# Splitting 1024-column weight units whole, the low part stored over the raw unit, in a one-layer diffusion block on Trainium2

## What is computed

```
mod = silu(c) @ w_ada + b_ada                       # six vectors: sh1 sc1 g1 sh2 sc2 g2
h   = modulate(rms_norm(x), sh1, sc1);  hc likewise for ctx
p   = h @ w_in ; pc = hc @ w_in                     # q, k, v of both head groups, rotary
x   = x + g1 * (concat(diff_attention, window_attention) @ w_out)
h2  = modulate(rms_norm(x), sh2, sc2)
q   = h2 @ peer_w_q ; top 16 of 128 x 128 keys per head -> experts, gates
x   = x + g2 * sum_e gate * gelu(h2 . u_e) * v_e
out = rms_norm(x)
```

## Time and profile before

| what | value |
|---|---|
| median of 3 runs | 2382.22 us (2380.1 to 2387.5) |
| the profiled execution | 2381.41 us |
| its span in the trace | 2379.6 us |
| PE busy | 2252.3 us, 95% of the span |
| DVE busy | 1640.9 us, 69% |
| ACT busy | 1220.5 us, 51% |
| POOL busy | 248.0 us, 10% |
| DMA | 453 MB, mean 190 GB/s |

### The profile page before, as it was taken

One profiled execution on the slowest core, in us unless ns is written; L12 is line 12 of the kernel. 1 busy time (PEld: TensorE's weight loads), 2 busy tenths in 40 slices (PEclk: granted clock), 3 DMA queues, 4 the chain that ended last, 5 costly groups with the idle time before them and its releaser, 6 DMA issues.

```text
span 2379.6 us, 43735 instructions
## 1 busy us (share of the span) xinstructions
PE 2252.3 (95%) x14034; PEld 1975.0 (83%) x14034; DVE 1640.9 (69%) x2935; ACT 1220.5 (51%) x2195; POOL 248.0 (10%) x152
## 2 busy tenths in 40 slices
PE   4899999579997999999999999999999999999997
PEld 1488887356897999999999999999888888888886
DVE  6387667776668878888868887877555555555555
ACT  2232244256444367677665555555555555555554
POOL 0000000920004610000111111111000000000000
PEclk8899999689998999999999999999999999999999
DMA  9878867310475745555554444444655555565552
GB/s 381 344 259 280 287 236 249 131 36 1 141 250 192 239 156 180 185 180 181 187 167 159 159 159 159 159 158 151 229 191 192 192 192 194 194 194 193 193 191 102
DMA packets 123895, 453.29 MB, mean 190 GB/s; under 512 B 14401, under 2 KB 15169, under 8 KB 123201
## 3 DMA queue, kind: packets, MB, share of 16 engines
q1 hardware_dynamic: 123840, 452.63, 56.3%
HBM read 448.38 MB, written 4.19 MB: 190 GB/s over the span
## 4 chain that ended last, share of the span: by engine, by line
PE 88%; DVE 7%; DMA 2%; issue 2%; ACT 1%; SPq 0%; DVEq 0%; ACTq 0%
PE PS L683 78%; PE PS L956 2%; PE PS L837 2%; DVE w_lo L1034 2%; DMA ada_t<-w_ada 1%; PE PS L811 1%; DVE pr L1258 1%; DVE st L1256 1%; PE PS L725 1%; PE PS L690 1%; PE PS L825 1%; PE PS L666 1%; DMA raw<-stream 1%; DVE yb L1070 0%; DVE st L1232 0%
## 5 line engine op out<-in xcount | busy, mean ns | idle before, releaser
L1034 DVE TENSOR_TENSOR w_lo<-raw,w_hi 128x512 fp32r<-128x512 f32 x1296 | 924.8, 723 | 566.5 <-ACT w_hi L373 551.2
L373 ACT ACTIVATE w_hi<-raw 128x512 fp32r<-128x512 f32 x1296 | 815.9, 630 | 912.6 <-PE PS L683 899.1
L683 PE MATMUL PS<-h_h,w_hi 128*128 128x256 f32 (+1 forms) x2304 | 661.7, 287 | 14.3 <-DVE w_lo L1034 14.3
L683 PE MATMUL PS<-h_l,w_hi 128*128 128x256 f32 (+1 forms) x2304 | 654.1, 284 | 0.0
L683 PE MATMUL PS<-h_h,w_lo 128*128 128x256 f32 (+1 forms) x2304 | 653.9, 284 | 0.0
L683 PEld LDWEIGHTS PS<-h_h,w_hi 128*128 128x128 f32 x2304 | 444.3, 193 | 16.9 <-DVE w_lo L1034 9.0
L683 PEld LDWEIGHTS PS<-h_l,w_hi 128*128 128x128 f32 x2304 | 444.6, 193 | 0.1
L683 PEld LDWEIGHTS PS<-h_h,w_lo 128*128 128x128 f32 x2304 | 444.2, 193 | 0.0
L683 PE MATMUL PS<-w_hi,p_hi 128*128 128x512 f32 x1024 | 398.5, 389 | 0.0
L683 PE MATMUL PS<-w_lo,p_hi 128*128 128x512 f32 x1024 | 398.3, 389 | 0.0
L683 PE MATMUL PS<-w_hi,p_lo 128*128 128x512 f32 x1024 | 398.3, 389 | 0.0
(11 more groups left out here) (192 smaller groups left out, 2465.3 us busy)
## 6 DMA issues: line engine op xcount, KB each, us to landing
raw<-stream SPq DMA_DIRECT2D x648, 512.0 KB, 3.4
ada<-w_ada SPq DMA_DIRECT2D x128, 512.0 KB, 4.6
ada_t<-w_ada SPq DMA_DIRECT2D x64, 512.0 KB, 9.5
x_c<-x_ctx SPq DMA_DIRECT2D x1, 2048.0 KB, 7.9
x<-x_lat SPq DMA_DIRECT2D x1, 2048.0 KB, 15.1
x_scratch<-x SPq DMA_DIRECT2D x1, 2048.0 KB, 7.3
x<-x_scratch SPq DMA_DIRECT2D x1, 2048.0 KB, 10.6
outT<-ot SPq DMA_DIRECT2D x4, 512.0 KB, 2.6
```

Of the source, the lines that this page charges most:

```text
L373: nc.scalar.activation(w_hi[:, (2 * j + hf) % SPLIT, :], raw[:, j, hf * HALF:(hf + 1) * HALF], ACT.Copy).then_inc(S["w_high"], 1)
L683: ins = mm(out_, l_, r_, start=(start and q == 0), stop=(stop and q == 2), skip_group_check=check)
L1034: V_.tensor_tensor(w_lo[:, h % SPLIT, :], raw[:, h // 2 % RAW, at_:at_ + HALF], w_hi[:, h % SPLIT, :].bitcast(F32), ALU.subtract).then_inc ...
```

## The change

ACT rounds a whole unit (1024 columns) in one instruction, and DVE makes its low part in one instruction. The low part is written over the raw unit: `w_lo` now lies at the address of `raw`. The memory that `w_lo` had goes to `w_hi`, so both rings hold eight halves (four units). Because the raw slot now holds the low part until PE has read it, SP issues the load of unit u only when PE has used unit u-4 (`w_free`), no longer when the low part of unit u-4 is made. The places where a half was split for each row or each third of a step (`modulate_and_split`, `next_low`) now split a unit at every second half.

```diff
-RAW, SPLIT, ADA, ADA1 = 4, 4, 4, 8
+RAW, SPLIT, ADA, ADA1 = 4, 8, 4, 8
...
-        w_lo = at("w_lo", [P, SPLIT, HALF], F32R, 24 * KB)
+        w_lo = at("w_lo", [P, SPLIT, HALF], F32R, 0)
...
                 if not first:
-                    sp.wait_ge(S["w_low"], 8 * b + 2 * (j - 3))
+                    sp.wait_ge(S["w_free"], 8 * b + 2 * (j + 1))
                 sp.dma_start(raw[:, j, :], stream[4 * b + j]).then_inc(raw_in[j], 16)
...
-            def half_high(b, j, hf):
-                act.wait_ge(S["w_free"], 8 * b + (2 * j + hf + 1))
-                nc.scalar.activation(w_hi[:, (2 * j + hf) % SPLIT, :], raw[:, j, hf * HALF:(hf + 1) * HALF],
-                                     ACT.Copy).then_inc(S["w_high"], 1)
-
             def split_high(b, j):
 
                 act.wait_ge(raw_in[j], 16 * b + 16)
-                half_high(b, j, 0)
-                half_high(b, j, 1)
+                act.wait_ge(S["w_free"], 8 * b + 2 * (j + 1))
+                nc.scalar.activation(w_hi[:, 2 * j:2 * j + 2, :].rearrange("p a n -> p (a n)"), raw[:, j, :], ACT.Copy
+                                     ).then_inc(S["w_high"], 2)
...
                 if k % 2 == 0:
-                    act.wait_ge(raw_in[k // 2 % RAW], 16 * (k // 8) + 16)
-                half_high(k // 8, k // 2 % RAW, k % 2)
+                    split_high(k // 8, k // 2 % RAW)
...
             def split_low(b, j):
-                half_low(b, 2 * j)
-                half_low(b, 2 * j + 1)
+
+                dve.wait_ge(S["w_high"], 8 * b + 2 * (j + 1))
+                V_.tensor_tensor(w_lo[:, 2 * j:2 * j + 2, :].rearrange("p a n -> p (a n)"), raw[:, j, :],
+                                 w_hi[:, 2 * j:2 * j + 2, :].rearrange("p a n -> p (a n)").bitcast(F32), ALU.subtract
+                                 ).then_inc(S["w_low"], 2)
...
                 modulate_low(k)
-                half_low(k // 8, k % 8)
+                if k % 2 == 0:
+                    split_low(k // 8, k // 2 % RAW)
...
                 for _ in range(n):
-                    half_low(half[0] // 8, half[0] % 8)
+                    if half[0] % 2 == 0:
+                        split_low(half[0] // 8, half[0] // 2 % RAW)
                     half[0] += 1
```

## The result

| what | before | changed |
|---|---|---|
| median | 2381.19 us of 4 runs (2380.1 to 2387.5) | 2404.86 us of 4 runs (2401.5 to 2409.44) |
| ratio | | 1.0095, 95% interval 1.0068 to 1.0123: slower, by about 1% |
| span of the profiled execution | 2379.6 us | 2406.0 us |

The page of the changed kernel: busy time by engine, then its two groups of splits (count, busy us, mean ns, idle before and its releaser; the ones to set beside them are in the earlier trace rows).

The account below looks back on a forecast made before the run. PE was taken to bound the kernel, busy 95% of the span. Terms 3.0 - 1.0 + 13.7 - 7.5 + 2.6 + 0.5 = +11.3 us on 2381.4 gave 2392.7, plus 0.8 for the median, rounded to 2394; range 2382 to 2403.

Parts of the forecast that it names:

- First chunk, +3.0: First chunk: PE's first half waits longer for a fresh whole unit in four groups; +3.0 us (1.5 to 4).
- Chunks 5 to 8, -1.0: Chunks 5 to 8: the deeper ring lets rotary work start earlier at chunk ends; -1.0 us (-2.5 to +1.5).
- Output projection, +13.7: Output projection: late `ada` load and sum delay low parts; PE stalls seven times 1.95 us, +13.7 us (10.9 to 18.6).
- The next pair arrives in time: Output projection: the pair after a stall was released before it, so the 1.95 us stall comes once in four units.
- Query projection, -7.5 and +2.6: Query projection: wider DVE turns and fewer waits, -7.5 us (-2 to -12); POOL's late last `ada` load at its end, +2.6.
- the 4.4 us: Query projection: what the wider DVE instruction recovers over some 40 halves that took 1.55 us against PE's 1.44.
- U and V, +0.5: U and V stages: 5.9 us to a ready unit fits in 8.2 us with little to spare; +0.5 us (0 to 3).
- Attention, 0: Attention, up to the first matmul of the output projection: forecast 0 us.
- the loose ring: Rival: `ada` lands in about 3.3 us, output projection term falls to 5; total +3, 2385 us; chance 0.22.
- The lock turns: Rival: 1024-column turns free the query projection of its waits, gaining some 20 us; about 2376 us; chance 0.08.
- loads did not bound the long stages: Denies the rival that landing over 6 us makes every ring slot late in the long stages: 2446 us; chance 0.05.

Follow-up runs that it names:

- e2: Kernel before, still with 512-column splits, but low part over the raw unit, rings of four units, load released by PE; 2390.84 us, ratio 1.0042.
- e6: Changed kernel with output projection `ada` loads one turn earlier, first chunk split by halves, `x2` read back in four pieces; 2375.97 us, ratio 0.9969.
- e3: Changed kernel with each `ada` load of the output projection one turn (two units) earlier in SP's queue; 2382.71 us, ratio 1.0006.
- e7: e3 with the `ada` loads of the query projection one turn earlier too; 2383.92 us, ratio 1.0.
- e4: Changed kernel with DVE's sum behind the two low parts of its turn in the output projection, SP's queue unchanged; 2382.11 us, ratio 1.0004.
- e5: e2 with the edit of e3, and `x2` read back in four pieces; 2374.28 us, ratio 0.9971.
- e8: e3 with the first four `ada` loads of column group 5 ahead of the loads of units 74 and 75; 2387.4 us, ratio 1.0014.
- e1: Kernel before with 1024-column splits, low parts in their own buffer, rings of two units, load released by the low part; 2492.73 us, ratio 1.0476.

## Why the prediction was wrong

The direction, the stage and the mechanism of the largest term were right; the size was half of what was measured, and the time (2404.86) fell just above the range (2382 to 2403). The output projection's term was too small by 8.0 us, more than half of the 15 us that are missing. By the steps of the prediction:

- **First chunk, +3.0: right.** Measured +3.1, shown to be the width's by e2 and e6.
- **Chunks 5 to 8, -1.0: the sign right, the size open.** It was -2.6. PE's wait for the turned queries fell from 6.2 to 4.2 us, and to 3.9 with halves (e2), so the gain of the deeper ring is there and larger than the 0.9 that I gave it. But e3, e7 and e4, which have the changed kernel's code there, show -2.4, -2.6 and +0.2; the granted clock of the stage was 0.96 in e4, 1.00 in the other three and 0.97 before the change. One trace does not settle a term of this size.
- **Output projection, +13.7: this is the step that failed, in size.** The period and the count held: the 28 units from 76 on are seven groups of four, and their waits are 1.79, 2.40, 2.18, 2.40, 2.08, 2.52 and 2.24 us, 2.23 in the mean where I had 1.95. That is 1.9 us in all. (By the prediction's own numbers the pair behind a stall has no slack, 7.7 us against 1.95 + 5.77. So between units 80 and 90 the loss of a group is split over its two pairs: 1.69 and 0.71, 0.82 and 1.36, 0.26 and 2.14. "The next pair arrives in time" was not right there, without changing the sum of a group.) The parts are not all right either: in the turn shown above the `ada` load left 0.86 us after PE's end with unit 77 (642.68), where I had 0.5, and landed in 4.2 us, where I had 4.5. The larger error is that a stall was priced at its length alone: the edges of ten waits are 2.5 us, and the lower clock behind three of them, less what the start of the stage lost before the change too, 4.1. Together these are 8.5 us for the 8.0 that the term was short. The prediction quoted the clock of 0.77 behind the gaps of the query projection and used it only for a rival; the term put both at nothing.
- **Query projection, -7.5 and +2.6: the sum near (-3.6 against -4.9), both parts wrong, which is luck.** PE's waits for low parts fell only from 14.3 to 11.0 us, and 2.0 of that came from the large stalls, where I had counted 3.1 (4.63 and 6.93 us before; 2.46, 2.64 and 4.46 now). The same code gave -6.5 in e3 and -5.6 in e4 for the norm and this stage. I expected that a DVE turn between two of GpSimd's would carry twice as many columns in the same time. The trace after, DVE first, then GpSimd:

```profile
809.13 58.59 DVE L1028 TENSOR_TENSOR w_lo<-raw,w_hi 128x1024 fp32r<-128x1024 f32 x19 [2.02 <-ACT w_hi L375]
```

```profile
811.08 3.27 POOL L346 TENSOR_TENSOR acc<-acc,ada 128x1024 f32<-128x1024 f32 x1
```

  19 units in 58.59 us are 3.08 us each. Before, 24 halves in 37.23 were 3.10 for a unit. GpSimd's sum, 2.70 us before, now takes 3.27, as it stands behind a longer instruction. The turns got wider for both, and the 4.4 us were not recovered. The late end cost nothing either: PE waited 1.9 us for the copies of the result, as before. The Trainium skill, SBUF — State Buffer, section "Who interferes with whom", says that the port pair which VectorE and GpSimd share is an exclusive lock, held for the whole of the instruction that came first; the trace agrees, now with GpSimd's 3.27 us as the number.
- **U and V, +0.5: low.** U was +0.2, with 0.6 us of waits for low parts in it. V was +2.3, of which 1.9 is the wait behind the read of `x2`, a DMA in SP's queue that I had not counted among the things that a unit load is late behind. That e5 and e6 bring the stage to +0.1 shows it.
- **Attention, 0:** +2.8 here, and between -1.6 and +3.5 in e3, e4 and e7 with the same code, so no finding about the change. The tail's +1.6 is 0.0 in e3, e4 and e7 and 1.7 in e8, whose code there is the same; its granted clock was 0.81 here and 0.86 before the change, and I read it the same way.

Of the rivals, the loose ring fell: `ada` landed in 4.1 us (median of 15, from 3.9 to 4.6), 0.4 less than before the change, and not in 3.3. The Trainium skill, SBUF — State Buffer, section "The DMA setup-cost knee", by whose fit the transfer alone would take an estimated 3.2 us, comes close for the unit loads of this kernel (3.3 by the page of the profile), and not for the `ada` load that follows two of them (4.1). The lock turns did not decide, and loads did not bound the long stages.

With the output projection's term as measured, 21.7 us, the prediction's sum is +19.3 us where the trace has +26.4. The 7.1 us that are left are U and V (2.0 more than forecast), the query projection (1.3), chunks 1 to 4 (0.9), the first chunk (0.1), and attention and tail (4.4), which differ between executions of one code, less 1.6 of chunks 5 to 8.

## What to carry to other kernels

When a buffer is written in place, its load is released by the last reader instead of the middle one, and everything that stands behind that load in the same queue moves with it: look there for another transfer that an engine needs before its next step on the buffer. Break such a dependency where the slack is cheapest; here moving each load, or each sum, by a turn gave back all 21.7 us. A wider instruction delays its first result and holds up the engine it excludes for longer, and in e1 it did not pay in a ring of two units. A wait of PE is priced with its edges and with the slower matmuls that may follow it: here 2.5 and 4.1 us beside 15.6.

## What was not expected of the hardware

- Behind three of ten PE waits, of 1.79, 2.52 and 2.24 us, the granted clock fell to 0.50 for 3.4 us; behind the other seven, of up to 2.14 us, it stayed at 1.00 through 75 us.
- The same code with the same busy time of PE (47.91 of 50 us) was granted 0.90 of the clock in one execution and 1.00 in another, and the attention stage differed by 5 us. A difference of that size in one pair of traces is no finding about a change.
- Whole units in a ring of two cost 110 us with ACT busy for 44% of the span and DVE for 64%: no share of busy time told of it.
